# Low moving parts of the expert tables and of the second query projection placed 192 bytes further behind the high ones

## The reference

```python
def peer(t, w_q, sub_keys, u_tab, v_tab):        # once in each block; 8 heads, 16 of 16384 experts
    q = t @ w_q                                  # 1024 x 2048
    s = scores of the two halves of q against 128 + 128 keys
    idx, g = the best 16 of the 16 x 16 pairs, and their softmax
    act = gelu(einsum(u_tab[idx], t))
    return einsum(g * act, v_tab[idx])
```

## The kernel before

| operand | used as | byte in the partition | modulo 512 |
|---|---|---|---|
| hl | weights of wq, u, v | 176256 | 128 |
| hsplit high, low | moving of u | 192640, 200832 | 128, 128 |
| csplit, slot c high, low | moving of v | 192640 + 2048 c, + 1024 | 128, 128 |
| raw_split high, low | moving of wq, block 2 | 28800, 36992 | 128, 128 |
| shifted_raw high, low, step k | moving of wq, block 1 | 77952 + 1040 k, 86272 + 1040 k | 128 + 16 k, 256 + 16 k |
| ring_lo, s_lo | low weights of the other projections | 4224, 28800 | 128, 128 |
| h_parts high, low | moving, block 1 | 45184, 53376 | 128, 128 |
| whi_front | high weights with h_parts | 61568 | 128 |
| og_hi, og_lo | moving, block 2 | 53888, 117824 | 128, 64 |
| mixed_hi, mixed_lo (block 2) | moving, block 2 | 85056, 127040 | 64, 64 |
| n_hi, n_lo, step k | moving, block 2 | 118336 + 1088 k, 127040 + 1088 k | 64 + 64 k |
| whi_a | high weights with og and mixed | 196992 | 384 |

## Time and profile before

### The profile page before, as it was taken

The page is one execution under the profiler, slowest core; times in us unless marked ns, Lnnn a source line. Parts: engine busy times, 40 slices in busy tenths (PEclk is TensorE's granted clock), DMA queues, the critical chain, the costliest instruction groups (busy, mean ns, idle before and its releaser), DMA issues.

```text
span 2256.0 us, 48254 instructions
## 1 busy us (share of the span) xinstructions
PE 2216.1 (98%) x15536; PEld 2038.1 (90%) x15536; DVE 1692.7 (75%) x3690; ACT 1306.0 (58%) x2727; POOL 436.4 (19%) x277
## 2 busy tenths in 40 slices
PE   8999999999999999999999999999999999999999
PEld 2788899999999888888889999999999999888888
DVE  4687768888879777777656875768888788777777
ACT  3567555555578555555554564655555587555554
POOL 0000000666664000000000000001767681000000
PEclk9999999999999999999999999999999999999999
DMA  8777545777764666666455434555777755666665
GB/s 312 246 241 235 178 152 186 185 179 186 178 152 126 210 209 209 208 208 208 160 169 160 159 110 143 196 160 185 178 186 185 180 131 153 213 215 212 211 214 170
DMA packets 191118, 422.88 MB, mean 187 GB/s; under 512 B 54288, under 2 KB 88336, under 8 KB 190624
## 3 DMA queue, kind: packets, MB, share of 16 engines
q1 hardware_dynamic: 150112, 413.73, 56.4%
q0 software_dynamic: 36864, 0.15, 4.6%
q10 hardware_dynamic: 4032, 7.64, 0.9%
HBM read 403.48 MB, written 17.96 MB: 187 GB/s over the span
## 4 chain that ended last, share of the span: by engine, by line
PE 92%; DVE 3%; ACT 2%; DMA 1%; issue 1%; POOL 0%; DVEq 0%; ACTq 0%; POOLq 0%
PE ps L2241 21%; PE ps L933 16%; PE ps L935 15%; PE ps L934 15%; PE ps L2242 11%; PE ps L958 6%; PE ps L2550 3%; PE ps L1864 1%; PE ps L1842 1%; DMA ring<-stream 1%; PE ps L2273 1%; PE ps L2164 1%; DVE ring_lo L612 1%; PE ps L1856 1%; ACT arena L677 0%
## 5 line engine op out<-in xcount | busy, mean ns | idle before, releaser
L2241 PE MATMUL ps<-csplit,hl 128*128 128x512 f32 x2048 | 717.4, 395 | 4.3 <-issue 3.4
L2474 POOL DMA_INDIRECT gates<-gbuf,picks_at x256 | 431.7, 1686 | 922.4 <-issue 483.8
L933 PE MATMUL ps<-hsplit,hl 128*128 128x256 f32 x2048 | 582.9, 285 | 0.0
L935 PE MATMUL ps<-hsplit,hl 128*128 128x256 f32 x2048 | 579.9, 283 | 0.0
L934 PE MATMUL ps<-hsplit,hl 128*128 128x256 f32 x2048 | 579.9, 283 | 0.0
L2242 PE MATMUL ps<-csplit,hl 128*128 128x256 f32 x2048 | 574.8, 281 | 0.0
L2317 ACT CAST hl<-ring 128x512 fp32r<-128x512 f32 x562 | 343.0, 620 | 297.6 <-PE ps L935 295.6
L2320 DVE TENSOR_TENSOR hl<-ring,hl 128x512 fp32r<-128x512 f32 x562 | 386.0, 693 | 122.9 <-ACT hl L2317 103.5
L2241 PEld LDWEIGHTS ps<-csplit,hl 128*128 128x128 f32 x2048 | 384.3, 188 | 94.6 <-issue 4.5
L2657 DVE TENSOR_TENSOR hl<-ring,hl 128x512 fp32r<-128x512 f32 x508 | 351.3, 692 | 73.0 <-ACT hl L2647 60.2
L934 PEld LDWEIGHTS ps<-hsplit,hl 128*128 128x128 f32 x2048 | 393.4, 192 | 0.0
(11 more groups left out here) (418 smaller groups left out, 3482.8 us busy)
## 6 DMA issues: line engine op xcount, KB each, us to landing
ring<-stream SPq DMA_DIRECT2D x675, 512.0 KB
s_area<-stream SPq DMA_DIRECT2D x48, 512.0 KB, 5.2
gates<-zeros SPq DMA_DIRECT2D x32, 512.0 KB, 5.1
gring<-gates SPq DMA_DIRECT2D x256, 64.0 KB, 3.2
gates<-gbuf,picks_at POOLq DMA_INDIRECT x256
arena<-xc ACTq DMA_DIRECT2D x2, 1024.0 KB, 15.4
arena<-keys ACTq DMA_DIRECT2D x2, 1024.0 KB, 7.6
gbuf<-consts ACTq DMA_DIRECT2D x1, 1120.0 KB, 5.3
```

Source lines behind the costliest of these rows:

```text
L933: pe.matmul(out_ap, w[0], m[0], start=start, stop=False)
L935: return pe.matmul(out_ap, w[0], m[1], start=False, stop=stop)
L2241: pe.matmul(ps[:, bank, :], w_hi, m_both, start=start, stop=False)
L2474: pool.indirect_dma_start(out=cells, out_offset=bass.IndirectOffsetOnAxis(ap=picks_at[:, i, c:c + 1], axis=0), in_=gates[:, i, c:c + 1], i ...
```

## The change

Three tensors get 48 elements (192 bytes) between the high and the low part. `hsplit` and `raw_split` are placed as two rows of 2048 + 48 elements, so the low part starts 8384 bytes behind the high one instead of 8192. `csplit` becomes a ring of eight pieces of 256 + 48 elements: each piece starts 1216 bytes behind the one before instead of 1024, and the moving operand of the 512-column matmul is two runs of 256 columns with a gap of 48 elements. The scratch space for the search over the keys starts 96 elements later. No instruction is added, removed or moved, and no wait changes.

```diff
-    hsplit, _ = place("hsplit", [P, 2, KD, T], F32R, at=gbuf_at + 2 * HLRING * HALF)
-    csplit, _ = place("csplit", [P, CRING, 2, T], F32R, at=gbuf_at + 2 * HLRING * HALF)
+    SHIFT = 48
+    hpair, _ = place("hsplit", [P, 2, KD * T + SHIFT], F32R, at=gbuf_at + 2 * HLRING * HALF)
+    hsplit = hpair[:, :, 0:KD * T].rearrange("p x (k t) -> p x k t", k=KD)
+    cpair, _ = place("csplit", [P, CRING, 2, T + SHIFT], F32R, at=gbuf_at + 2 * HLRING * HALF)
+    csplit = cpair[:, :, :, 0:T]
...
-    K.take(8192)
+    K.take(8192 + 2 * SHIFT)
...
-    raw_split, _ = place("raw_split", [P, 2, KD, T], F32R, at=s_at)
+    rpair, _ = place("raw_split", [P, 2, KD * T + SHIFT], F32R, at=s_at)
+    raw_split = rpair[:, :, 0:KD * T].rearrange("p x (k t) -> p x k t", k=KD)
```

## The result

The changed kernel takes 2234.85 us (median of 4 runs, 2231.95 to 2238.73), the kernel before 2258.99 us (median of 4, 2256.55 to 2262.76). The ratio is 0.9893, with a 95% interval of 0.9869 to 0.9917: 24 us less, where 13 were forecast. The profiled execution took 2233.44 us with a span of 2231.6.

A forecast was written before the change was run, and what follows sets the result against it. It took the distance between TensorE's matmul starts, times their number, as the bound in `u` and `v`. Terms 11.8 (`u`) + 0.8 (`wq` of block 2) + 0 (`v`) = 12.6 us off the median 2261.38 gave 2248.8, forecast 2248; range 2234 to 2263.

The forecast's parts named there:

- the price of `og`: Gain per triple of matmuls in `u`, taken from the nearest profiled tensor: 6.6 ns, bounds zero and 10 ns.
- The count of 2376 matmuls in 280 us: Sign of being right: stretches of `u` hold some 2376 matmuls in 280 us instead of 2336.
- `wq` of block 2: Term for 128 triples on `raw_split`, at 6.6 ns each: 0.8 us less.
- The rule against it: Skill page's rule that weight loads take no read bandwidth from the running matmul, so addresses can't matter: zero gain.
- no address effect: Rival for `u`: columns and weight load alone set the matmul distance; time 2261 us, chance 0.15.
- The last 16 units: End of `u` in both blocks, 256 triples: VectorE would be the next to be late, so no gain counted.
- For `v` as a whole I take no change.: Both `v` loops: new relative places and two-run operand together count 0; places alone bounded at 14 us either way.
- The term of 0: The share of the `v` loops in the forecast sum: 0 us.
- the sign that `v` gains: More than 1733 matmuls in 300 us of `v` would show a gain there.
- `v` gains as well: Rival: slots leaving difference 0 speed up `v` by 7 to 14 us more, 2241 down to 2234; chance 0.18.
- The jump costs: Rival: second run of each 512-column matmul in `v` costs 7 to 14 ns a pair, 2262 to 2276 us; chance 0.17.

The follow-up runs named there:

- whole_shift: Both parts of `hsplit` moved 192 bytes further behind `hl`, without a gap between them, against the kernel before; 2240.05 us.
- the best version: `csplit` as in the changed kernel, `hsplit` and `raw_split` shifted whole by 192 bytes without a gap; 2226.38 us, ratio 0.9867 to the kernel before.
- before_again: The kernel before, run again unchanged; 2261.06 us.
- both_shift: `hl`, `hsplit` and `csplit` all moved 192 bytes further on against the kernel before, so no relative place changes; 2254.31 us.
- u_only: Only the gaps in `hsplit` and `raw_split`, with `csplit` as in the kernel before; 2241.30 us, ratio 0.9936.
- `v` alone: Only `csplit` as in the changed kernel, the rest as in the kernel before; 2247.93 us, ratio 0.9960.
- v_jump_timed: Only `csplit` changed against the kernel before: 512 bytes between its pieces, relative places modulo 512 kept; 2259.91 us, ratio 1.0003.

## Why the prediction was right about `u` and wrong about the size

**`u`, right.** Forecast 6.6 ns on 1792 triples, 11.8 us; measured 2 x 5.94 = 11.9 us. The size came out right by some luck in the choice of the neighbour. I took the price of `og` although its differences were 0, 256, 320 against 0, 0, 320. With the period of 256 bytes these are the same places, 0, 0, 64, and I didn't know that. The price isn't one of having left 0, as I had it: the table above has 350.0, 356.0 or 340.0 ns for other places. `mixed` shows how far it could have gone wrong: modulo 256 it has the places of `whole_shift` (64, 64, 64), where 353.3 and 340.0 ns were both measured. The count of 2376 matmuls in 280 us was 2380, the loads went to 188 ns. `wq` of block 2 gained 0.83 us where 0.8 was forecast, with triples of 353.3 ns; with `raw_split` unchanged it took 46.9 to 47.6 us in other profiles, so the last digit means little.

**The rule against it.** By the page "TensorE: Matmul & The Clock Gate" of the Trainium skill (section "Step-by-step: what each phase is for") the two reads have ports of their own and the next weights cost the running matmul nothing. 120.0 ns with the operands in step, 120.0 again with both shifted, and 113.3 with one of them shifted speak against it for this pattern: a load beside every matmul, with 256 columns of four bytes. The measurement decides. The rival "no address effect" is out.

**The last 16 units, nearly right in size and wrong in the reason.** I counted nothing, as VectorE would be the next to be late, and they gave 0.53 and 0.22 us. The rows reach past the last matmul of `u` (in block 2 it starts at 1894.0 us) into the wait for `v`. Two stretches that lie wholly in the last 16 units of block 2, of the kernel before and then of the changed one, columns as there:

```profile
1850.00:1890.00 40.00, 40.00 (x345) 40.00 (x344) 40.00 (x92) 36.86 (x106) 16.96 (x10) 1.00 0.45 120
```

```profile
1825.00:1865.00 40.00, 40.00 (x349) 40.00 (x349) 40.00 (x93) 37.20 (x107) 23.33 (x13) 1.00 0.48 120
```

VectorE is busy all the time in both, and still 40 us hold 349 matmuls instead of 345. By the starts the units without the wait behind them take 72.0 us instead of 72.7 in each block, most of the 0.85 us that 128 x 6.7 ns make. What takes it back is the wait for the first matmul of `v`, which grew from 1.9 and 2.0 us to 2.1 and 2.5. In the best version 40 us hold 349 matmuls again, though every second unit or so has triples of 340 ns; that VectorE sets the pace there is possible and not shown.

**`v`, wrong.** The step that failed is this: "For `v` as a whole I take no change." The term of 0 measured 8.6 to 9 us. Its error lies one step earlier. I read 353 ns in block 1 and 346 in block 2 as two speeds of one layout, and took the difference as a measure of my ignorance, 14 us either way. I didn't ask which of the two a next execution would have. Of the ten `v` loops with the old relative place of `csplit` that were profiled (the two of before, `before_again`, `whole_shift`, `both_shift` and `u_only`), five ran at 353.3 and five at 346.7 over their first 1008 pairs, and seven changed to the other value for the last 16. The mean, 350.0, is what the median of many runs holds, and not one profile. The text named more than 1733 matmuls in 300 us as the sign that `v` gains; with 1736 and 1737 the sign was there, though only block 1 shows how large the gain is. The change makes a pair 345.8 in every loop seen: 4.2 ns x 2048 = 8.6 us. `v` alone measured 0.40%, 9.0 us. The sum by the measured terms is 11.9 + 0.8 + 0.75 + 8.6 = 22.1 us, against 1.04% of 2258.53, 23.5 us, with an interval of 19 to 28.

**The rivals.** "`v` gains as well" came true, at 2241 to 2234 us; the measured 2234.85 is at its far end. Its condition was wrong in the same way as the sum: not block 1 gains 7 ns, but whichever loop had drawn the slow value. "The jump costs" is refuted by `v_jump_timed`: its upper bound of 1.002 is 4.5 us on 2048 pairs, 2.2 ns each, where the rival had 7 to 14.

**The single profile misleads twice.** It held 6.0 us of clock at the start that the change didn't make, and it hid part of the gain in `v`, as its block 2 had drawn the fast value. In block 2 the changed kernel even looks 0.7 us slower, since in that execution the clock fell for 3.4 us at the start of `v`, behind a wait of 2.5 us. Block 1 had the same fall behind a wait of 2.1 us (11 matmuls in 3.4 us at a granted clock of 0.50). The first 4 us or so of block 2, in the changed kernel and then in the kernel before:

```profile
1870.80:1875.00 4.20, 4.15 (x17) 3.62 (x18) 2.90 (x7) 1.66 (x4) 0.00 (x0) 0.68 0.49 155
```

```profile
1896.00:1900.00 4.00, 4.00 (x23) 3.54 (x24) 3.23 (x7) 2.39 (x5) 0.00 (x0) 1.00 0.44 139
```

The second profile of the changed kernel has neither, after waits of 2.3 us: `v` took 354.9 us in each block from its first start to its last, where the slow pace of before took 362.4 and the fast one 355.8.

**What stays open.** Why the stream settles on one of two patterns and keeps it until the next break, and why a gap of 192 bytes holds the fast one where a gap of 512 doesn't; the shifts other than 192 in `v`, which were seen once each and not timed; why a shift of 192 is the best in `u` and brings nothing in `v`. That SBUF reads collide was argued from the relative place and the period, and not seen. A version with the gates started earlier, so that the faster `u` keeps its 23 us, wasn't tried.

## What to carry to other kernels

Where matmuls follow one another without a wait and each has a weight load beside it, try moving one operand by 32 to 224 bytes relative to the other: it costs a line, and here it made the spacing shorter by up to 5.6%, with the best place found only by trying. Before a forecast from one profile, run the kernel unchanged once more and compare stage by stage; two speeds of one loop with the same addresses are a draw that a layout may hold or lose. Compare the pace ahead of a break in the stream with the pace behind it too, and take the wait at a seam out of a stage before judging what limits the stage. And look at the stage behind the one that gets faster, since what it waits for (here the gates' transfers) takes its share back, with a drop of the clock on top.

## What the runs showed of the hardware that I had not expected

- The distance between matmuls of 256 columns in the rounded float32 form depends on the place of the moving operand relative to the weights loaded meanwhile: 120.0 ns at 0 bytes, 113.3 at 192, 116.7 to 118.7 at the others modulo 256 (120.0 over most of the loop at 384), all of it in keeping with a period of 256 bytes.
- Moving both together changes nothing: 324.65 us for 112 units before, and 324.65 with all three tensors 192 bytes on.
- One loop of one program can run at two speeds, 353.3 or 346.7 ns a pair, and keeps its own for 1008 pairs, some 350 us. Behind a break of some 75 ns it can have the other: in seven of ten loops here. In `u` a shift of 192 bytes went from 340.0 to 353.3 ns a triple at such a break.
- A moving operand in two runs, 512 bytes apart, costs nothing that can be measured: ratio 1.0003 (0.9986 to 1.002).
- The first 270 us of the program, untouched, took from 267.3 to 274.1 us, with the granted clock at 0.57 and 0.53 in two stretches of 7 us or at 1.00.
